# Attention's inverse sums by way of memory, the residual's first third loaded alone, and the next weights split in attention's last pair

## Time and profile before

| | us |
|---|---|
| three timed runs | 3409.95, 3421.74, 3426.02 |
| their median | 3421.74 |
| profiled execution | 3412.66 |
| its span, first to last instruction | 3411.0 |
| mean granted clock of PE | 0.981 of full speed |

### The profile page before, as it was taken

How to read it: one execution, slowest core, us unless ns; L and a number is a source line. 1 busy time by engine, 2 the same in 40 slices (tenths; PEclk the granted TensorE clock), 3 DMA queues, 4 the chain that set the end, 5 groups by cost and what they waited for, 6 DMA issues and landing times. The chain is left out here.

```text
span 3411.0 us, 62772 instructions
## 1 busy us (share of the span) xinstructions
PE 3258.8 (96%) x26834; PEld 3042.0 (89%) x26834; DVE 1319.3 (39%) x1721; ACT 717.4 (21%) x1238; POOL 1037.1 (30%) x678
## 2 busy tenths in 40 slices
PE   7999978888799999999999999999999999999997
PEld 7988857777799999999999997677799999999997
DVE  5640055556543333333335110266533333333333
ACT  3212133344331000000002001366421000000004
POOL 4453053442203232222224341011233232222223
PEclk8999978999899999999999999999999999999999
DMA  6232143334712111111110233465311111111101
GB/s 204 79 98 75 47 126 120 122 105 145 230 32 68 37 37 38 42 55 43 43 37 31 94 103 125 160 223 178 105 50 56 37 37 43 39 53 43 43 25 56
DMA packets 277229, 279.97 MB, mean 82 GB/s; under 512 B 24328, under 2 KB 236897, under 8 KB 276024
## 3 DMA queue, kind: packets, MB, share of 16 engines
q1 hardware_dynamic: 269912, 250.98, 22.6%
q0 software_dynamic: 7136, 26.35, 2.5%
HBM read 208.48 MB, written 70.90 MB: 82 GB/s over the span
## 5 line engine op out<-in xcount | busy, mean ns | idle before, releaser
L405 PE MATMUL PS<-hT_high,w_split_tiles 128*128 128x384 f32 x5856 | 1189.0, 335 | 3.6 <-DVEq L1320 2.6
L405 PEld LDWEIGHTS PS<-hT_high,w_split_tiles 128*128 128x128 f32 x5856 | 1029.3, 188 | 5.8 <-POOLq L1190 2.9
L405 PE MATMUL PS<-hT_low,w_split_tiles 128*128 128x384 f32 x2928 | 665.6, 335 | 0.0
L405 PE MATMUL PS<-ffn_act_split,w_down_split 128*128 128x384 f32 x3024 | 529.1, 334 | 2.6 <-DVE ffn_act_split L877 1.6
L405 PEld LDWEIGHTS PS<-ffn_act_split,w_down_split 128*128 128x128 f32 x3024 | 524.3, 188 | 4.4 <-DVE xT L860 2.3
L405 PEld LDWEIGHTS PS<-hT_low,w_split_tiles 128*128 128x128 f32 x2928 | 522.6, 188 | 0.0
L860 DVE TENSOR_TENSOR xT<-xT,PS 128x1152 f32<-128x1152 f32 x168 | 227.4, 1354 | 285.4 <-PE PS L405 285.2
L585 POOL CAST w_split_tiles<-w_raw_tiles 128x1024 fp32r<-128x1024 f32 x44 | 46.9, 1066 | 439.8 <-PE PS L405 321.1
L585 POOL CAST w_split_tiles<-attention_oT 128x1024 fp32r<-128x1024 f32 x42 | 43.7, 1040 | 333.1 <-PE PS L405 313.1
L800 ACT CAST ffn_act_split<-ffn_room 128x1152 fp32r<-128x1152 f32 x22 | 25.5, 1161 | 483.2 <-PE PS L405 347.8
L800 ACT CAST ffn_act_split<-attention_oT 128x1152 fp32r<-128x1152 f32 x22 | 25.5, 1161 | 478.5 <-PE PS L405 347.8
(11 more groups left out here) (449 smaller groups left out, 4756.5 us busy)
## 6 DMA issues: line engine op xcount, KB each, us to landing
w_raw_tiles<-in_ffn_w_gu_dram SPq DMA_DIRECT2D x44, 512.0 KB, 3.9
attention_oT<-in_ffn_w_gu_dram SPq DMA_DIRECT2D x44, 512.0 KB, 3.9
cache_kT<-kT_dram SPq DMA_DIRECT2D x8, 2048.0 KB, 11.7
cache_v<-in_cache_c_v_dram SPq DMA_DIRECT2D x64, 256.0 KB, 4.6
ffn_room<-in_ffn_w_down_dram SPq DMA_DIRECT2D x11, 1024.0 KB, 5.9
attention_oT<-in_ffn_w_down_dram SPq DMA_DIRECT2D x11, 1024.0 KB, 5.8
rest_dram<-w_raw_tiles SPq DMA_DIRECT2D x36, 256.0 KB, 2.1
w_raw_tiles<-in_c_w_qkv_dram POOLq DMA_DIRECT2D x18, 512.0 KB, 4.6
```

Of the source, the lines that this page charges most:

```text
L405: m = nc.tensor.matmul(PS[:, banks + j, 0:GN], wl if p == 2 else wh, sl if p == 1 else sh, start=(k == first and p == 0), stop=(k == last ...
```

## The change

- Mixer's residual stage: SP loads weights 0 to 3, then row tile 3, weights 4 and 5, the first third (group 0's columns) of xT's block 0, and weights 6 and 7; the thirds of blocks 1 and 2 go between state stores, those of 3 to 7 follow row tile 4, and the other two thirds of each block follow when its first has been added. The weights' raw memory moves by one block. Tile 3's square and root go behind ACT's fifth weight, its sums and gate ahead of DVE's first add. Product banks go from three to four.
- Attention, pairs 0 to 6: PE no longer spreads the inverse sums. DVE writes them to `inv`, and evicts v's product by a copy. SP stores a pair's 2 x 1024 inverses to memory as single floats, waits for them, and loads them back, each row repeated over 64 partitions, in two halves of 512 columns; POOL multiplies `oT` by each half. The second half's load waits for the first half's multiply. The last pair (pair 7) works as before.
- Attention's last pair also loads the first two weight tiles of the output projection into memory that pair 6's queries and keys held; POOL splits them. The projection then begins with four warming calls.

```diff
--- before.py
+++ after.py
@@ -991,8 +991,6 @@
...
-        for s in range(2):
-            sp.dma_start(raw[:, s], wv[:, :, s * P:(s + 1) * P]).then_inc(w_in[s], 16)
@@ -1009,8 +1007,8 @@
...
-        for n in range(KT):
-            split_tile(e, pool, n // 2, n % 2, raw, ws, w_in, mm, high, split)
+        for n in range(2, KT):
+            split_tile(e, pool, n // 2, n % 2, raw, ws, w_in, mm, high, split, 1)
@@ -1035,7 +1033,7 @@
...
-        e.keep_warm(10)
+        e.keep_warm(4)
@@ -1107,6 +1105,10 @@
...
+    def pool_credits(pool):
+        pool.sem_inc(high, 2)
+        pool.sem_inc(split, 2)
@@ -1879,10 +1881,16 @@
...
-                ahead.load_weights(sp)
+                ahead.load_weights(sp, 0, 4)
+                ahead.load_rows(sp, 3)
+                ahead.load_weights(sp, 4, 6)
+                ahead.load_x(sp, 0, 0)
+                ahead.load_weights(sp, 6, KT)
...
                 store_rows(s)
...
+                ahead.load_x(sp, 1, 0)
             if s == 1:
@@ -1906,6 +1914,7 @@
...
+        ahead.load_x(sp, 2, 0)
@@ -2930,7 +2939,7 @@
...
-        return PS[:, (j * KT + n) % 3, 0:GN]
+        return PS[:, (j * KT + n) % 4, 0:GN]
@@ -2947,9 +2956,18 @@
...
+    def load_x(sp, n, part_):
+        c = slice(GN, T) if part_ else group(0)
+        read = -(-(n * T + c.stop - D) // D)
+        if read > 0:
+            sp.wait_ge(w_low, read)
+        if part_:
+            sp.wait_ge(added, n + 1)
+        sp.dma_start(xT[:, n, c], e.scr["xT"][n * P:(n + 1) * P, c]).then_inc(x_in[n], 16)
@@ -3018,15 +3036,18 @@
...
     def sync(sp):
-        load_rows(sp, TPG)
         load_rows(sp, TPG + 1)
+        for n in range(3, KT):
+            load_x(sp, n, 0)
+        load_rows(sp, TPG + 2)
         for n in range(KT):
-            sp.wait_ge(w_low, min(n + 2, KT))
-            sp.dma_start(xT[:, n], e.scr["xT"][n * P:(n + 1) * P]).then_inc(x_in[n], 16)
-        for t in range(TPG + 2, NT):
+            load_x(sp, n, 1)
+            if n == 4:
+                load_rows(sp, 2 * TPG)
+        for t in range(2 * TPG + 1, NT):
             load_rows(sp, t)
@@ -3041,8 +3062,10 @@
...
-            if j * KT + n >= 3:
-                pe.wait_ge(added, j * KT + n - 2)
+            if j == 0 and n == 3:
+                ahead.done.banks_read(pe)
+            if j * KT + n >= 4:
+                pe.wait_ge(added, j * KT + n - 3)
@@ -3055,7 +3078,7 @@
...
-        e.keep_warm(2, 3)
+        e.keep_warm(2)
@@ -3070,9 +3093,12 @@
...
+            if n == 4:
+                square_o(act, TPG)
+                root(act, TPG)
@@ -3084,8 +3110,8 @@
...
-            if j == 0:
-                dve.wait_ge(x_in[n], 16)
+            if j < 2:
+                dve.wait_ge(x_in[n], 16 * (j + 1))
@@ -3096,17 +3122,20 @@
...
+        sums(dve, TPG)
+        norm_gate(dve, TPG)
@@ -3440,12 +3472,17 @@
...
-    def turned_blocks(t):
-
-        return 2 * blocks(t) + (t < NPT)
...
+    def summed(g):
+
+        i, t, u = step(g)
+        return i == NPAIR - 1 and t < NPT
+
+    def turned_blocks(g):
+
+        return 2 * blocks(step(g)[1]) + summed(g)
@@ -3500,12 +3541,31 @@
...
+        def out_raw(n):
+
+            return (qh, kh)[n][:, NPAIR % 2, 0:D].rearrange("p (k c) -> p k c", k=KT)
...
+            def spread_sums(i):
+
+                sp.wait_ge(sum_inv, i * STEPS + NPT)
+                for hp in range(2):
+                    sp.dma_start(e.scr["inv"][i, hp].rearrange("(t p) -> p t", p=P), inv[:, i % 2, hp], allow_slow_non_contiguous=True
+                                 ).then_inc(inv_out, 16)
+                sp.wait_ge(inv_out, 32 * (i + 1))
+                for x in range(2):
+                    if i or x:
+                        sp.wait_ge(scaled, 2 * i + x)
+                    c_ = slice(x * (LP // 2), (x + 1) * (LP // 2))
+                    for hp in range(2):
+                        sp.dma_start(wide[hp * HD:(hp + 1) * HD], e.scr["inv"][i, hp:hp + 1, c_].broadcast_to((HD, LP // 2))
+                                     ).then_inc(wide_in, 16)
+
             for i in range(NPAIR):
@@ -3517,6 +3577,8 @@
...
+                if i >= 2:
+                    spread_sums(i - 2)
@@ -3526,6 +3588,10 @@
...
+            for n in range(2):
+                sp.dma_start(out_raw(n), w_out.rearrange("(k p) n -> p k n", p=P)[:, :, n * P:(n + 1) * P]
+                             ).then_inc(out_w_in[n], 16)
+            spread_sums(NPAIR - 2)
@@ -3574,7 +3640,7 @@
...
-                order = [(hp, j) for hp in range(2) for j in range(n)] + [("sums", 0)] * (t < NPT)
+                order = [(hp, j) for hp in range(2) for j in range(n)] + [("sums", 0)] * summed(g)
@@ -3698,11 +3764,26 @@
...
+            def scale(i):
+                for x in range(2):
+                    c_ = slice(x * (LP // 2), (x + 1) * (LP // 2))
+                    pool.wait_ge(wide_in, 32 * (2 * i + x + 1))
+                    pool.wait_ge(o_kept, i * STEPS + NPT)
+                    nc.gpsimd.tensor_tensor(oT[:, i, c_], oT[:, i, c_], wide[:], ALU.mult).then_inc(scaled, 1)
+
...
                     prepare(i + 1)
+                    if i:
+                        scale(i - 1)
+            for n in range(2):
+                pool.wait_ge(out_w_in[n], 16)
+                nc.gpsimd.tensor_copy(w_first[:, n, 0], out_raw(n)).then_inc(out_w_high, 1)
+                pool.wait_ge(out_w_high, n + 1)
+                nc.gpsimd.tensor_tensor(w_first[:, n, 1], out_raw(n), w_first[:, n, 0], ALU.subtract).then_inc(out_w_low, 1)
+            scale(NPAIR - 2)

@@ -3725,24 +3806,32 @@
...
-                v.reciprocal(rs[:, g % 2], sm[:, g % 2]).then_inc(sum_inv, 1)
+                i, t, u = step(g)
+                if t == SAMPLE or summed(g):
+                    v.reciprocal(rs[:, g % 2], sm[:, g % 2]).then_inc(sum_inv, 1)
+                else:
+                    if i >= 2:
+                        dve.wait_ge(inv_out, 32 * (i - 1))
+                    v.reciprocal(inv[:, i % 2, :, t:t + 1], sm[:, g % 2]).then_inc(sum_inv, 1)
...

                 i, t, u = step(g)
                 dve.wait_ge(o_mm, g + 1)
@@ -3887,16 +3976,17 @@
...
-            attention(e, oT)
+            keys_at = e.place() + KEYS_AT
+            w = e.at("w_split_tiles", [P, 2, 2, KT, P], keys_at, F32R)
+            attention(e, oT, w, d["c_w_out"][0])
...
-                first_raw = e.at("w_out_raw", [P, 2, KT, P], e.place())
-                wd = e.sb(last, "w_down_split", [P, 2, 2, D], F32R)
+                first_raw = e.at("w_out_raw", [P, 2, KT, P], keys_at + 16 * KT * P)
+                wd = e.at("w_down_split", [P, 2, 2, D], keys_at + 16 * KT * P, F32R)
```

More of the change, by code:

```diff
@@ L1885, in turn @@
                 store_rows(s)
+            if s == NT - 1:
+                ahead.load_x(sp, 1, 0)
             if s == 1:
@@ L2876, with __init__ @@
 class Ahead:
-    def __init__(self, load_rows, load_gains, load_weights, turn, square, root, high, weight, sums, gate, low):
-        self.load_rows, self.load_gains, self.load_weights = load_rows, load_gains, load_weights
+    def __init__(self, load_rows, load_gains, load_weights, load_x, turn, square, root, high, weight, sums, gate, low):
+        self.load_rows, self.load_gains, self.load_weights, self.load_x = load_rows, load_gains, load_weights, load_x
         self.turn, self.square, self.root, self.high, self.weight = turn, square, root, high, weight
@@ L2948, in load_gains, with load_weights @@
                 sp.dma_start(gain[r * DK:(r + 1) * DK, m:m + 1], head_gain.rearrange("n c -> c n")).then_inc(gain_in, 16)
-    def load_weights(sp):
-        for n in range(KT):
+    def load_weights(sp, first, end):
+        for n in range(first, end):
             sp.dma_start(w_raw[:, n], wv[:, :, n * P:(n + 1) * P]).then_inc(w_in[n], 16)
+    def load_x(sp, n, part_):
[6 more added lines that the diff above has]
+        sp.dma_start(xT[:, n, c], e.scr["xT"][n * P:(n + 1) * P, c]).then_inc(x_in[n], 16)
     def turn(pe, t):
@@ L3101, in vector @@
                 t = tiles(j + 1)[(n - 1) // 2] if j + 1 < G and 0 < n < 7 else None
-                if t is not None and n % 2:
+                made = t == TPG and n % 2
+                if t is not None and n % 2 and not made:
                     sums(dve, t)
@@ L3108, in vector @@
                     add_square(j - 1, KT - 1)
-                if t is not None:
+                if t is not None and not made:
                     if n % 2:
@@ L3417, in _, with attention @@
                                      ).then_inc(copied, 1)
-def attention(e, oT):
+KEYS_AT = 94432
+def attention(e, oT, w_first, w_out):
     nc, d, PS, ident, c = e.nc, e.d, e.PS, e.ident, e.const
@@ L3459, in attention @@
             engine_of.append("dve")
-        for n in range(chunks(t)):
+        for n in range(chunks(g)):
             chunk_of["probs", g, n] = len(engine_of)
@@ L3483, in attention @@
         so = e.sb(ctx, "sample_o", [P, 2 * P])
+        inv = e.sb(ctx, "pair_sums_inv", [P, 2, 2, NPT])
```

(9 more changed lines are left out.)

29 lines of the change are left out of this document (15 added, 14 removed).

## The result

The changed kernel takes 3441.53 us, the median of six runs (3436.17 to 3459.62); the kernel before, six runs in all now, takes 3419.11. The ratio is 1.0082, 95% interval 1.0064 to 1.0101: **slower, by 22 us between the medians** and by 22 to 35 us by the interval, where I had forecast 20 us faster, and outside my range of 3381 to 3416. Timed again later, it came to 1.0088 (1.0053 to 1.0123).

The account below looks back on a forecast made before the run. PE was taken to bound the kernel, with SP taking its place in attention. Residual stage -13.0, next weights -4.8 and inverse sums -2.2 made -20 us, from 3417.6 to 3397.6 us; range 3381 to 3416 us.

Parts of the forecast that it names:

- What bounds the kernel, and PE's share: Whole kernel: PE is busy 3258.8 of 3411.0 us, so only its idle time or removed PE work counts.
- Residual stage, -13.0: Mixer: PE's 11.05 us pause and 2.6 us of slow clock go, 0.6 given back for tile 4.
- R4: Rival, residual stage: the pause only moves to tile 4, keeping 6 of 13 us; 3405 us, chance 0.08.
- Next weights, -4.8: Output projection: first product comes sooner with two weight tiles split in attention; -4.8 at DVE's fast end, -3.7 at its slow.
- Inverse sums, -2.2: Attention: SP's store-and-reload chain replaces PE as the bound, so only pair 0 keeps its gain, -2.2 us.
- X: Attention: time of a pair's two stores of 1024 single floats, taken as 2.4 us, between 0.8 and 9.6.
- The halves, 4.85: Attention: bias rows landing 2.65, POOL's first multiply with hand-over 1.3, second half's issue 0.9; together 4.85 us.
- C: Attention: SP's chain per pair, 24.6 + 2.4 + 4.85 = 31.85 us; six periods take 5 C + 29.9 = 189.2 us.
- 5 X - 32: Whole change: the summed gain in us written by the stores' time X; about -20 at the forecast's 2.4.
- R3: Rival, attention: at X = 9.6 SP, q and k, and POOL's end come late; +27, 3445 us, chance 0.10.
- R2: Rival, attention: single floats cost more per piece; X = 5 gives 3411 us, 3 to 8 no measurable change; chance 0.22.
- R1: Rival, attention: the chain stays hidden, X near 0.8, pairs of 29.4 to 30.5; 3385 to 3390 us, chance 0.18.

Follow-up runs that it names:

- best version: Changed kernel with rows of 8 floats, stores ahead of cache_v, wide halves around cache_kT, DVE's sample-query copy in the eighth step: 3390.61 us, 0.9928 of the kernel before.
- rows of 8: Changed kernel with inverses stored as 128 pieces of 32 bytes per head, not 1024 single floats, POOL reading in the other order: 3404.26 us, 0.9957 of the kernel before.

## Why the prediction was wrong, point by point

- **What bounds the kernel, and PE's share.** Right. The first pair, with no chain yet, took PE 29.65 us (2181.03 to 2210.68), and the best version's shortest periods are this long, 29.6: PE's own 29.4 with little on top.
- **Residual stage, -13.0.** Right in mechanism and size: -12.5 in the trace, and 14.4 us in times for this part alone. Ahead of group 1's first turn PE no longer waits. The 0.6 us that I gave back for tile 4 was 0.93:

```profile
912.68 1.09 PE L2982 MATMUL PS<-consts_f,mix_rows 128*128 128x128 f32 x8 [0.93 <-DVE mix_rows L3029]
```

  R4, a pause that only moves, falls. Not in my sum: in the traces 0.5 us (residual part alone), 3.8 us (changed kernel) and 3.9 us (sums on PE) come back in the first FFN and 1.6 in the v projection (below).
- **Next weights, -4.8.** Right: 11.89 to 6.83 us, -5.1, with the sums on PE. The fast end of DVE's pace was the one to take: with POOL idle, its eight low parts took 10.24 us there, 1.28 each, where beside POOL's split they took 16.29, and PE ran through product 0 without a wait. PE's own pace of 1.6 us for nine matmuls was right (1.56), though the row that I gave for it, 19 in 3.00 us, would make 1.42. The times don't show the gain (0.9956 without it, 0.9962 with it, each 0.0015 to either side). In the changed kernel it is lost, since PE waits 9.5 us ahead of its warming matmuls, until POOL's last multiply is done.
- **Inverse sums, -2.2: the step that failed.** That SP takes PE's place with a chain behind cache_kT was right. A chain as long as I took it, with rows of 8, has the forecast's period (31.1 to 32.0 us), by two errors that cancel: X near 0 and longer halves. In all it gave -13.7 us and not -20; most of the gap is the 5.4 us of the first FFN and the v projection. The mis-sized term is X, the two stores of 1024 single floats. I took 2.4 us, "as the number of pieces is the same" as in the row of 256-byte pieces. From the stores' issue to the wide loads it took 16.4 to 17.5 us in the changed kernel, where my terms give 11.7 - 1.0 + 2.4 = 13.1: X was about 6.4, and more in other executions. The number of pieces was the wrong likeness: as many floats 64 bytes apart cost 2 us a chain, and close together 7. My row had neither the size of the pieces nor the nearness of their targets.
- **The halves, 4.85.** Measured 6.0 to 6.9 us from the first wide load to the next cache_v: half of it issue time, and a hand-over to POOL and back that I had at 0. That is 1.4 us a chain, 7 us over five.
- **The sum in terms of X.** With C = 37.7 my 5 C + 29.9 gives 218.4 us for six periods, 29.1 more than before, and 27 with the first pair's gain; the trace has 31.8. Of the 5 us between, 3.3 lie in the six periods (221.66 us by PE's first scores) and 1.4 in the last pair; their cause stays open. At X = 6.4 my "5 X - 32" is 0. It lacked the halves' 7 us, those 5 us, the 8.5 that POOL's late end costs (+3.4 in place of -5.1), and the 5.4 of the first FFN and the v projection: 26 us, where the trace has 28 without the 15.2 and the 2.5 at its ends.
- **R3** was the case that came true: SP reaches each pair late, q and k are late, DVE waits for k, POOL ends the stage. (DVE's wait for the stores was in no rival.) It had the size at the end right (8 us; POOL's last multiply ended at 2472.1, 8.0 behind PE). Only its price was put at X = 9.6, and I wrote that the gain would be gone from 6.4 on, while at 6.4 the kernel was slower by 22 us or more. So I gave the right mechanism 0.10, because I set its threshold too high: the end effects belonged into the sum for every chain longer than PE's pair, not only into its worst case.
- **R2** had the price (X from 3 to 8) and a wrong time for it, for the same reason. **R1** needed X near 0.8. Rows of 8 had less than that and still no period of 29.4 to 30.5, because of the longer halves.
- **The pages.** The warning that I left beside R3 (the Trainium skill, DMA: Bandwidth & Descriptors; the sentence stands in its section "Rules for kernel authors": a non-contiguous last dimension becomes one descriptor per element) pointed at the right place, and rows of 8 against single floats show what that choice costs here: 37 us. The number of elements alone is the smaller part of it, as the floats 64 bytes apart show. The fixed 2.0 us of the same page ("Anatomy of one DMA", whose fit is for DMAs issued from GpSimd, where SP issues these) doesn't explain the delay: it would be the same for 256 pieces and for 2048, and store to wide was 10.8 and 17.5 us.

## What to carry to other kernels

When a value per partition has to go through memory, lay it out so that each partition writes its own contiguous run, and let the engine that reads it do the permuting: here this took 37 us off, for a POOL multiply of 1.54 us in place of 1.27. Before putting a store and its reload on a queue that also feeds other engines, write down what stands behind each wait and how long the chain is against the pace of the bounding engine; a chain that is only level with it already gives back nearly everything (3.2 us of attention were left of the 15.1 that I had counted as PE's saving). And a small transfer waited for behind a 2 MB load should go ahead of it: here this, with the stores moved ahead too, took attention from 270.50 to 265.20 us.

## What the runs showed of the hardware that I had not expected

- 2048 four-byte writes into 8 KB of memory leave the queue within 2 us, and for 6 to 10 us after that both their report and the loads behind them are held up (0 and then 35 to 44 GB/s, where the fastest kernel's cache_v loads at the same place move 261).

```profile
2278.00:2280.00 2.00, 2.00 (x28) 1.50 (x23) 1.67 (x8) 1.80 (x5) 0.00 (x0) 1.00 0.87 261
```

- The same number of writes 64 bytes apart, and so spread over 16 times the memory, cost 2 us per chain and not 7. That writes into one line wait for one another would explain it; what happens inside the memory no run here shows, and 64 bytes was the only distance tried.
- With a pause taken out of one stage, a slow clock showed up in the next. In the changed kernel PE was busy without a pause until 998.37, paused 2.0 us as before, and then ran on the 1.2 GHz level until about 1011, which the kernel before did not do there. Of the 13 profiles with the residual part 12 had a dip there, of differing length. Why, and whether the pause taken out brings it, stays open.

```profile
1000.00:1005.00 5.00, 4.63 (x13) 2.91 (x14) 2.81 (x3) 2.40 (x2) 0.52 (x1) 0.60 0.72 203
1005.00:1010.00 5.00, 5.00 (x14) 3.44 (x15) 1.58 (x2) 2.81 (x4) 4.64 (x4) 0.50 0.12 33
```

- The 5282 matmuls of the projection and the second FFN took 916 us in most profiles and 931 to 934 in four, at a granted clock of 1.00 in both. The changed kernel shows both values. All four are profiles of kernels that store single floats, of which there are seven; the seven profiles without such stores all have 916 to 919. Whether that is chance no run here settles.
